# Triangular inverses from R and its transpose, and overflow rows in pairs of weight pieces, in an RWKV-7 and experts block

## What is computed

```python
def step(S, inp):                                   # time mixing, per token
    sa = jnp.einsum('bhij,bhj->bhi', S, -kk_t)
    S = (S * w_t[:, :, None, :] + sa[..., None] * (kk_t * a_t)[:, :, None, :]
         + v_t[..., None] * k_t[:, :, None, :])
    y_t = jnp.einsum('bhij,bhj->bhi', S, r_t)
...
def expert_block(args):                             # experts, per block of rows
    xb = xf[toks]
    gt = jnp.minimum(xb @ w_e_gate[e] + b_e_gate[e], SWIGLU_LIMIT)
    up = jnp.clip(xb @ w_e_up[e] + b_e_up[e], -SWIGLU_LIMIT, SWIGLU_LIMIT)
    act = (up + 1.0) * (gt * jax.nn.sigmoid(gt * SWIGLU_ALPHA))
    return (act @ w_e_down[e] + b_e_down[e]) * wts[:, None]
```

## Time and profile before

| what | value |
|---|---|
| time, median of 3 runs | 3196.18 us (3189.34 to 3200.56) |
| the profiled execution's own time | 3188.35 us |
| its span in the profile | 3186.4 us |
| TensorE matmul busy / VectorE / ScalarE / GpSimd | 2842.3 / 1918.3 / 1259.2 / 263.4 us |
| granted TensorE clock, mean | 0.951 of full |
| first inversion, first product to the product behind "xa" | 176.19 to 255.62 us |
| wide rounds / narrow rounds | about 1644 to 2325 / 2325 to 3090 us |

### The profile page before, as it was taken

The page is one execution under the profiler, slowest core; times in us unless marked ns, Lnnn a source line. Parts: engine busy times, 40 slices in busy tenths (PEclk is TensorE's granted clock), DMA queues, the critical chain, the costliest instruction groups (busy, mean ns, idle before and its releaser), DMA issues.

```text
span 3186.4 us, 56497 instructions
## 1 busy us (share of the span) xinstructions
PE 2842.3 (89%) x21829; PEld 2368.1 (74%) x21829; DVE 1918.3 (60%) x2115; ACT 1259.2 (40%) x1359; POOL 263.4 (8%) x283
## 2 busy tenths in 40 slices
PE   6998999989899999899159999999999999999970
PEld 5787887978898999744147777777778888888860
DVE  3464646656432211112536767676789999999978
ACT  2302103030122111011125555555567777777751
POOL 1000000000000000000421010101000110001114
PEclk9999999999999999999579999999999999999985
DMA  9000000000011111131237777777789999999998
GB/s 330 22 2 8 14 2 21 2 15 8 2 33 46 40 53 46 49 92 37 85 124 264 260 264 260 263 261 264 259 338 379 376 378 384 383 376 378 382 326 235
DMA packets 149059, 562.46 MB, mean 177 GB/s; under 512 B 19400, under 2 KB 73056, under 8 KB 93650
## 3 DMA queue, kind: packets, MB, share of 16 engines
q1 hardware_dynamic: 124449, 503.18, 43.6%
q0 software_dynamic: 15440, 38.14, 4.1%
q10 hardware_dynamic: 9056, 19.54, 1.6%
HBM read 513.10 MB, written 47.70 MB: 176 GB/s over the span
## 4 chain that ended last, share of the span: by engine, by line
PE 78%; issue 11%; DVE 5%; POOL 3%; DMA 2%; ACT 1%; SPq 0%; DVEq 0%; POOLq 0%; ACTq 0%
PE bank L829 30%; PE bank L1872 12%; PE bank L1873 12%; PE bank L1874 12%; PE bank L1881 5%; PE bank L825 2%; PE bank L1850 2%; POOL rowtok_d L1382 1%; POOL y_got L1446 1%; PE bank L1860 1%; PE bank L1908 1%; DMA y_got<-ys_d,dest 1%; PE bank L1887 1%; DVE P L603 1%; PE bank L880 1%
## 5 line engine op out<-in xcount | busy, mean ns | idle before, releaser
L1709 DVE TENSOR_TENSOR w_lo<-raw_first,w_hi 128x2048 fp32r<-128x2048 f32 x275 | 619.0, 2283 | 76.7 <-ACT w_hi L1487 76.7
L1487 ACT ACTIVATE w_hi<-raw_first 128x2048 fp32r<-128x2048 f32 x276 | 528.2, 1918 | 262.8 <-PE bank L1881 81.9
L1872 PE MATMUL bank<-w_hi,x_hi 128*128 128x512 f32 x1088 | 439.3, 404 | 3.4 <-ACT yo_rows L1529 3.4
L1873 PE MATMUL bank<-w_lo,x_hi 128*128 128x512 f32 x1088 | 426.1, 392 | 0.0
L1874 PE MATMUL bank<-w_hi,x_lo 128*128 128x512 f32 x1088 | 425.6, 391 | 0.0
L1709 DVE TENSOR_TENSOR w_lo<-raw_rest,w_hi 128x2048 fp32r<-128x2048 f32 x136 | 307.6, 2283 | 24.7 <-ACT w_hi L1487 24.7
L1487 ACT ACTIVATE w_hi<-raw_rest 128x2048 fp32r<-128x2048 f32 x136 | 257.3, 1915 | 120.8 <-PE bank L1887 34.9
L829 PE MATMUL bank<-xm_hi,ring_hi 128*128 128x260 f32 x896 | 261.4, 292 | 17.3 <-DVE dz L781 8.2
L829 PE MATMUL bank<-xm_hi,ring_lo 128*128 128x260 f32 x896 | 254.6, 284 | 0.0
L829 PE MATMUL bank<-xm_lo,ring_hi 128*128 128x260 f32 x896 | 254.5, 284 | 0.0
L1872 PEld LDWEIGHTS bank<-w_hi,x_hi 128*128 128x128 f32 x1088 | 206.0, 189 | 58.6 <-issue 19.2
(11 more groups left out here) (347 smaller groups left out, 4684.2 us busy)
## 6 DMA issues: line engine op xcount, KB each, us to landing
raw_first<-in_w_e_up SPq DMA_DIRECT2D x138, 1024.0 KB, 6.4
raw_first<-in_w_e_gate SPq DMA_DIRECT2D x70, 1024.0 KB, 6.6
raw_rest<-in_w_e_gate SPq DMA_DIRECT2D x70, 1024.0 KB, 4.9
raw_first<-in_w_e_down SPq DMA_DIRECT2D x68, 1024.0 KB, 8.8
raw_rest<-in_w_e_down SPq DMA_DIRECT2D x68, 1024.0 KB, 8.2
ring<-in_w_in SPq DMA_DIRECT2D x40, 512.0 KB, 4.0
ys_d<-ar SPq DMA_DIRECT2D x18, 1024.0 KB
ys_d<-y_rows ACTq DMA_DIRECT2D x34, 512.0 KB, 8.8
```

What stands on the lines that cost most here:

```text
L1487: nc.scalar.activation(w_hi[:, j % NRING, :, :], raw_piece(j), ACT.Copy).then_inc(hi_done, 1)
L1709: nc.vector.tensor_tensor(w_lo[:, j % NRING, :, :], raw_piece(j), w_hi[:, j % NRING, :, :].bitcast(f32), ALU.subtract).then_inc(lo_done, 1)
L1872: nc.tensor.matmul(ps[:, :], hi, w_hi[:, slot, k, :], start=start and k == 0, stop=False)
L1873: nc.tensor.matmul(ps[:, :], hi, w_lo[:, slot, k, :], start=False, stop=False)
```

## The change

Inversion: the product for `Tm` is dropped; instead TensorE transposes the new `Rm` (4 transposes per block, "X"), and ScalarE copies the result into `Tm`. Level 0 takes no product: GpSimd multiplies `AT` by a mask (`M0`) and adds the identity (`R0`), block by block as VectorE finishes `AT`. Level 6 is computed on its one non-zero block only (columns 0 to 63 against 64 to 103), with VectorE copies. Levels 1 to 6 are one list of 30 steps, so the pipeline is not drained between levels: TensorE issues P of step i, D of step i-1, X of step i-2. "xa" is moved ahead of the inversion.

Experts: the overflow products of two pieces are issued together after the second piece, and have a semaphore of their own, `ov_used`, which now frees the raw slots (the queue of SyncE waits for it). `piece_used` is given right after the full products.

```diff
+    PE_J += [('xa', g) for g in range(3)] + [('X', 0, b) for b in range(NB)]
+    STEPS = [(l, b) for l in range(1, LEVELS) for b in range(NB)]
+    for i in range(len(STEPS) + 2):
+        if i < len(STEPS):
+            PE_J.append(('P',) + STEPS[i])
+        if 1 <= i <= len(STEPS):
+            PE_J.append(('D',) + STEPS[i - 1])
+        if i >= 2 and STEPS[i - 2][0] < LEVELS - 1:
+            PE_J.append(('X',) + STEPS[i - 2])
...
-            dve_j.done(pool, 'v', j, pool_passed)
-            for m, x in ((Tm, 'T0'), (Rm, 'R0')):
-                pool_j.mark(nc.gpsimd.tensor_copy(m[:, :, :], ident[0:TP, 0:TP].unsqueeze(1).to_broadcast([TP, NU, TP])), x)
+            for b in range(NB):
+                dve_j.done(pool, ('A', 4 * b + 3), j, pool_passed)
+                part = slice(4 * b, 4 * b + 4)
+                pool_j.mark(nc.gpsimd.tensor_tensor(Tm[:, part, :], AT[:, part, 0, :], m0t[:, 0:TP].unsqueeze(1).to_broadcast([TP, 4, TP]),
+                                                    ALU.mult), ('M0', b))
+                pool_j.done(pool, ('M0', b), j, pool_passed)
+                pool_j.mark(nc.gpsimd.tensor_tensor(Rm[:, part, :], Tm[:, part, :], ident[0:TP, 0:TP].unsqueeze(1).to_broadcast([TP, 4, TP]),
+                                                    ALU.add), ('R0', b))
...
+            for i, (l, b) in enumerate((l, b) for l in range(LEVELS - 1) for b in range(NB)):
+                pe_j.done(act, ('X', l, b), j)
+                act_j.mark(nc.scalar.activation(Tm[:, 4 * b:4 * b + 4, :], bank[6 + i % 2][0:TP, 0:4 * TP].rearrange(
+                    "p (u n) -> p u n", n=TP), ACT.Copy), ('T', l, b))
...
-            for l in range(LEVELS):
...
+            for i in range(len(STEPS) + 1):
+                if i < len(STEPS):
+                    l, b = STEPS[i]
+                    pe_j.done(dve, ('P', l, b), j)
+                    if i >= 2:
+                        pe_j.done(dve, ('D',) + STEPS[i - 2], j)
+                    src = bank[2 + i % 2]
+                    if l == LEVELS - 1:
+                        dve_j.mark(nc.vector.tensor_copy(P1[HS:TP, i % 2, :, 0:HS], src[HS:TP, 0:4 * HS].rearrange("p (m t) -> p m t", m=4)),
+                                   ('P', l, b))
+                    else:
+                        tt(('P', l, b), P1[:, i % 2, :, :], src[0:TP, 0:4 * TP].rearrange("p (m t) -> p m t", m=4),
                            mlev[:, l, 0:TP].unsqueeze(1).to_broadcast([TP, 4, TP]), ALU.mult)
-                    if s > 0:
-                        b = s - 1
-                        pe_j.done(dve, ('D', l, b), j)
-                        if l > 0:
-                            dve_j.done(dve, ('R', l - 1, b), j)
-                        else:
-                            pool_j.done(dve, 'R0', j)
-                        for x, m, bk in (('T', Tm, 4), ('R', Rm, 6)):
-                            if l == LEVELS - 1 and x == 'T':
-                                continue
-                            new = bank[bk + b % 2][0:TP, 0:4 * TP].rearrange("p (m t) -> p m t", m=4)
-                            if l == 0 and x == 'T':
-
-                                new = P1[:, b % 2, :, :]
-                                dve_j.done(dve, ('P', l, b), j)
-                            tt((x, l, b), m[:, 4 * b:4 * b + 4, :], new, m[:, 4 * b:4 * b + 4, :], ALU.add)
+                if i >= 1:
+                    l, b = STEPS[i - 1]
+                    pe_j.done(dve, ('D', l, b), j)
+                    src = bank[4 + (i - 1) % 2]
+                    if l == LEVELS - 1:
+                        dve_j.mark(nc.vector.tensor_copy(Rm[0:HS, 4 * b:4 * b + 4, HS:TP],
+                                                         src[0:HS, 0:4 * (TP - HS)].rearrange("p (m t) -> p m t", m=4)), ('R', l, b))
+                    else:
+                        tt(('R', l, b), Rm[:, 4 * b:4 * b + 4, :], src[0:TP, 0:4 * TP].rearrange("p (m t) -> p m t", m=4),
...
-            pool_j.done(pe, 'R0', j)
-            for l in range(LEVELS):
-                for s in range(NB + 1):
-                    if s < NB:
-                        if l > 0:
-                            dve_j.done(pe, ('T', l - 1, s), j)
-                            if s < 2:
-                                dve_j.done(pe, ('P', l - 1, 4 - s), j)
-                        if s >= 2:
-                            dve_j.done(pe, ('P', l, s - 2), j)
-                        for m in range(4):
-                            u = 4 * s + m
-                            ins = mm(bank[2 + s % 2][0:TP, TP * m:TP * (m + 1)], AT[:, u, 0, :], Tm[:, u, :])
-                        pe_j.mark(ins, ('P', l, s))
-                    if s > 0:
-                        b = s - 1
-                        dve_j.done(pe, ('P', l, b), j)
-                        if b >= 2:
-                            dve_j.done(pe, ('R', l, b - 2), j)
-                        elif l > 0:
-                            dve_j.done(pe, ('R', l - 1, 4 - b), j)
-                        for m in range(4):
-                            u = 4 * b + m
-                            if 0 < l < LEVELS - 1:
-                                mm(bank[4 + b % 2][0:TP, TP * m:TP * (m + 1)], Rm[:, u, :], P1[:, b % 2, m, :])
-                            ins = mm(bank[6 + b % 2][0:TP, TP * m:TP * (m + 1)], P1[:, b % 2, m, :], Rm[:, u, :])
-                        pe_j.mark(ins, ('D', l, b))
...
+            def transpose_r(i, l, b):
+                if i >= 2:
+                    act_j.done(pe, ('T', (i - 2) // NB, (i - 2) % NB), j)
+                for m in range(4):
+                    ins = nc.tensor.transpose(bank[6 + i % 2][0:TP, TP * m:TP * (m + 1)], Rm[:, 4 * b + m, :], ident[0:TP, 0:TP])
+                pe_j.mark(ins, ('X', l, b))
+
+            for b in range(NB):
+                pool_j.done(pe, ('R0', b), j)
+                transpose_r(b, 0, b)
+            act_j.done(pe, ('xa', 2), j)
+            for i in range(len(STEPS) + 2):
+                if i < len(STEPS):
+                    l, b = STEPS[i]
+                    act_j.done(pe, ('T', l - 1, b), j)
+                    if i >= 2:
+                        dve_j.done(pe, ('P',) + STEPS[i - 2], j, pe_passed if l == LEVELS - 1 else None)
+                    for m in range(4):
+                        u = 4 * b + m
+                        if l == LEVELS - 1:
+                            ins = mm(bank[2 + i % 2][HS:TP, HS * m:HS * (m + 1)], AT[0:HS, u, 0, HS:TP], Tm[0:HS, u, 0:HS])
+                        else:
+                            ins = mm(bank[2 + i % 2][0:TP, TP * m:TP * (m + 1)], AT[:, u, 0, :], Tm[:, u, :])
+                    pe_j.mark(ins, ('P', l, b))
+                if 1 <= i <= len(STEPS):
+                    l, b = STEPS[i - 1]
+                    dve_j.done(pe, ('P', l, b), j, pe_passed if l == LEVELS - 1 else None)
+                    for m in range(4):
+                        u = 4 * b + m
+                        if l == LEVELS - 1:
+                            n = TP - HS
+                            ins = mm(bank[4 + (i - 1) % 2][0:HS, n * m:n * (m + 1)], P1[HS:TP, (i - 1) % 2, m, 0:HS], Rm[HS:TP, u, HS:TP])
+                        else:
+                            ins = mm(bank[4 + (i - 1) % 2][0:TP, TP * m:TP * (m + 1)], P1[:, (i - 1) % 2, m, :], Rm[:, u, :])
+                    pe_j.mark(ins, ('D', l, b))
+                if i >= 2 and STEPS[i - 2][0] < LEVELS - 1:
+                    l, b = STEPS[i - 2]
+                    dve_j.done(pe, ('R', l, b), j)
+                    transpose_r(NB * l + b, l, b)
...
-                sp.wait_ge(piece_used, n + 1 - NRAW + NRING)
+                sp.wait_ge(ov_used, n + 1 - NRAW)
...
-                        if wide:
-                            nc.scalar.activation(yo_rows[:, n, :], ov_ps[n][:, 0:128], ACT.Copy).then_inc(y_read[1], 1)
+                        if wide and j == 11:
+                            act.wait_ge(ov_used, r * NPIECE + NPIECE)
+                            for n in range(2):
+                                nc.scalar.activation(yo_rows[:, n, :], ov_ps[n][:, 0:128], ACT.Copy).then_inc(y_read[1], 1)
...
+                            if t == 1:
+                                dve.wait_ge(ov_used, r * NPIECE + j + 1)
...
-                    if wide:
-                        if j == 0:
+                    ins.then_inc(piece_used, 1)
+                    if wide and j % 2 == 1:
+                        if j == 1:
                             for f in range(2):
                                 pe.wait_ge(xov_done[f], r + 1)
-                        if j in (0, 2):
+                        if j in (1, 3):
                             pe.wait_ge(y_read[1], r * 2 + 1 + j // 2)
-                        if j % 2 == 0:
-                            pe.wait_ge(gu_read[1], r * 4 + g + 1)
-                        ins = ov_products(ov_ps[g % 2], x_ov, j, HK * (j % 2), j % 2 == 0, False)
-                        if j % 2 == 1:
```

(43 more changed lines are left out.)

30 lines of the change are left out of this document (7 added, 23 removed).

## The result

The changed kernel takes 3112.72 us (median of 4 runs, 3108.64 to 3121.29) against 3194.61 for the kernel before in the same job (4 runs): a ratio of 0.9744, 95% interval 0.9723 to 0.9765. That is 82 us less, where 107 were forecast. The profiled execution took 3114.73 us for a span of 3113.1, against 3188.35 and 3186.4 before: 73.6 us less. The mean granted clock went down, from 0.951 to 0.938.

The account below looks back on a forecast made before the run. TensorE's number of products was taken to bound the inversion and the wide rounds; 76 + 31 = 107 us off 3188.35 gives 3081, as a median 3089 us; own range 3075 to 3105, with rivals 3062 to 3125.

Parts of the forecast that it names:

- The inversion, 76 forecast: Stretch from "xa" to "xc": 60.4 us instead of 79.4, 19.0 saved per pass, 76 us in four passes.
- 1, level 0 with "xa": Inversion start: "xa" lasts 3.8 us, GpSimd and transposes follow, level 1 starts 6.6 us after "xa" starts.
- TensorE at its low level: Rival, inversion levels 1 to 5: transposes drop the clock to 1.2 GHz, 191 us lost, 3280 in all; chance 0.04.
- Step 2: Inversion levels 1 to 5: 25 steps of P, D and 4 transposes at 1.91 us, 47.8 us per pass.
- Step 3: Inversion level 6 on its small block: 6.0 us per pass, bounds 4.5 to 8.1.
- GpSimd late: Rival, level 0 of the inversion: GpSimd operations take 2 us, 22 us lost, 3111; chance 0.08.
- dear transposes: Rival, inversion steps: a transpose group costs 0.73 us like a product, 28 us lost, 3117; chance 0.05.
- The wide rounds, 31 forecast: Experts' wide rounds: pairing overflow products saves 2.4 us per round, 31 us over 13 rounds.
- piece 10: Wide rounds, transposes around `u_ov`: 2.06 us becomes 1.29 with 16 products, 0.77 us saved per round.
- VectorE and ScalarE wait for loads: Rival, wide rounds: waits on pairs of loads give back the 31 us, 3120; chance 0.10.
- The price of a visit: Wide rounds: coming to and going from overflow products costs 0.39 us, saved for each whole visit dropped.

Follow-up runs that it names:

- one_x: `combo` with one transpose in place of four per step at levels 1 to 5, so the inverse is wrong; 3054.1 us, ratio 0.9559.
- xa_early: The changed kernel with each group of "xa" waiting only for its own `AT` instead of the last one; 3083.63 us, ratio 0.9656.
- xa_wide: The changed kernel with its idle time kept and "xa" products 104 columns wide instead of 64, but the last of each group; 3091.87 us, ratio 0.967.
- xov_first: The changed kernel with ScalarE copying `x_ov` before `a_ov` in piece 9 instead of after it; 3104.26 us, ratio 0.972.
- the runs of the halves: Against the kernel before (3193.86 us): the new inversion alone, 3129.77 us, and the paired overflow products alone, 3178.01 us.
- combo: The changed kernel with the edits of `xa_early` and `xov_first` together; 3073.07 us, ratio 0.9612.
- y_fill: `combo` with eight products `Vt` by `AT` put ahead of each of two TensorE waits, for the last `Rm` and the last `X`; 3074.8 us, ratio 0.9616.
- combo_l6: `combo` with level 6 of the inversion at full size instead of its one block; 3083.55 us, ratio 0.9642.
- y_in_s_l6: `combo` with products `Vt` by `AT` between the recurrence's steps and level 6 at full size; 3081.92 us, ratio 0.9651.

## Why the prediction was right in kind and 25 us too high in gain

**Bound and place: right.** TensorE's count of operations set the inversion (`one_x` shows it) and, but for one wait, the wide rounds, and both halves paid.

**The inversion, 76 forecast, 64 measured. The step that failed is 1, level 0 with "xa".** Its mechanism and its 6.6 us hold at full clock (6.4 in `xa_early`). But its 3.8 us for "xa" came from the earlier trace rows, behind 75 us of dense products; at its new place it stands behind an idle time of 1.12 us, and the clock fell for 10 to 14 us. From "xa" to "xc" that cost 20 us over four passes: 251.6 against 231.9 in `xa_wide`, which keeps the idle time, and whose median is 21 us lower. The rival "TensorE at its low level" named the right danger at the wrong place: I looked for it in the steps with their transposes and costed it there at 191 us, and did not ask it of the moved "xa". The nearest row, even showed an idle time of this length without a fall, so rows of before would have cleared it wrongly; what had changed was what followed. The number came out nearer than this mechanism deserves: at full clock the stretch is 57.9 us, not 60.4, and these 10 us over four passes hid half of the loss. That was luck.

**Step 2, 47.8 forecast, 45.0 measured** (186.08 to 231.09). The transposes cost the 0.36 of the earlier trace rows, not the 0.45 of the narrow rounds: 25 x 0.09 = 2.3 us per pass better. Two of the transposes' groups of level 5 lie behind 231.09, among level 6, so the split between steps 2 and 3 is rough. The steps ran at granted clock 1.00 from 188 on. The Trainium skill, "TensorE: Matmul & The Clock Gate", Part 4, has transposes not count as a busy TensorE. The steps, a fifth of whose time is transposes (0.36 of 1.82 us), show no fall, which leaves the rule open; the rise from 0.50 with transposes alone in the earlier trace rows speaks against it, and the two falls that the change brought followed products.

**Step 3, 6.0 forecast, 7.07 measured**, within its bounds. Not in the sum at all: the low clock behind level 6, 1.5 us in the first pass from "xc" to `m` (8.98 against 7.48) and 6.1 in the four. With it the profile gives 317.7 - 251.6 - 6.1 = 60 us for the inversion.

**GpSimd: right that it is off the path.** 1.06 us per operation where 0.9 was taken; the estimate of 0.91 from the Trainium skill's GPSIMD Engine Reference, section 3.1, is 14% low by this row. The rivals "GpSimd late" (2 us per operation) and "dear transposes" (0.73 per group) are refuted by the 1.06 and the 0.36 us.

**The wide rounds, 31 forecast, 16 to 18 measured. The failing term is piece 10, taken as 0.77 us saved.** It saved nothing: 1.28 us and the 16 products' 0.84, now elsewhere, are 2.12 against 2.06 before. I removed the 16 products from between the transpose of `u_ov` and the next ones as if nothing else had used that time; ScalarE's two copies had. With ScalarE's order changed the 1.28 became 0.46, and the 12.4 rounds between the marks save 27.8 us in the profile (16 + 8.5, so about 24, by the medians for all 13). "VectorE and ScalarE wait for loads", the rival that was to take the gain, did not come: between the first and the last transpose of `u_ov` loads end waits of ScalarE, none of TensorE. The price of a visit holds: in `xov_first` the pair of piece 1 lies between two full products 2.65 us apart and the next comes after 0.34. Less the bias row (0.23) and the two intervals of 0.228 it costs 2.30, and single visits cost 1.23 + 1.44 = 2.67 by the forecast's terms; so 0.37 saved, for 0.39:

```profile
1687.64 0.39 PE L1910 MATMUL bank<-w_hi,x_lo 128*128 128x512 f32 x1
1687.87 0.40 PE L1944 MATMUL bank<-bias_t,kind_row 128*128 128x512 f32 x1
1688.19 1.95 PE L1917 MATMUL bank<-raw_first,x_ov 128*32 128x128 f32 x64
1689.96 0.40 PE L1923 MATMUL bank<-bias_t,kind_ov 128*32 128x128 f32 x8
1690.29 0.50 PE L1908 MATMUL bank<-w_hi,x_hi 128*128 128x512 f32 x1
```

**Range.** The measured 3113 lies outside the forecast's own 3075 to 3105 and inside 3062 to 3125 only because rivals had stretched that. It lies where two of them would have put it (3111, 3117), by neither of their mechanisms: luck, too. Only the runs of the halves and of the two waits told this.

## What to carry to other kernels

A duration read at one place holds at another only if the granted clock does, so look at what idle time will come to lie ahead of moved work, and read the clock of the result first. When products are taken from between two operations, ask which other engine's copies they had hidden, and in what order that engine makes them. And cost a small block by its waits, and by the clock behind it, as well as by its columns: the full level 6 took only 2.2 us more per pass than the small one and gave that back behind it, though both kernels with it came out 10 us slower for a reason not found.

## What the runs showed of the hardware that was not expected

- An idle 1.12 us followed by "xa" in products of 64 columns (20 products, 40 records) took the granted clock from 1.00 to 0.50 for 10 to 14 us; the same idle time followed by products of 104 columns left it at 1.00, and so did those of 64 columns with no idle time ahead.
- fp32 products of 64 and of 104 columns with 104 rows took the same: 3.88 and 3.87 us for the 20, at granted clock 1.00. Cutting the moved columns bought nothing there. The 20 products `Vt` by `AT` have the 64-wide side stationary and move 104 columns, and take 2.00 us for as many records (at 266.64 in the kernel before, at 250.68 in the changed one), half as much. Turning the operands of "xa" round was not tried.
- Level 6 in small products (64x64 and 40x40) is followed by a granted clock of 0.50 to 0.57 (in three passes of four in the changed kernel, in all four of `combo`), and in `y_fill` without the two waits too (0.53); full products at that place keep it at 1.00 in all eight passes of `combo_l6` and `y_in_s_l6`.
- Transposes of 104x104 in fp32 cost 0.09 us each between products at full clock, and a fifth of them in the stream didn't lower it.
